# Attention's 32 modulation tiles on VectorE instead of TensorE, values and sums taken out by ScalarE, division by pairs of heads

## The reference, cut to what matters

```python
silu_c, silu_cc = jax.nn.silu(c), jax.nn.silu(c_ctx)
for layer in range(DEPTH):
    mod = jnp.split((silu_c @ w_mod[layer] + b_mod[layer])[:, None, :], 6, axis=-1)
    mod_c = jnp.split((silu_cc @ w_mod[layer] + b_mod[layer])[None, None, :], 6, axis=-1)
    ...
    # attention, 8 heads of 64 values; latents read context and latents, context reads context
    s = jnp.einsum('bhqd,bhkd->bhqk', q, k) * (B_QK ** -0.5)
    p = jax.nn.softmax(s, axis=-1)
    o = jnp.einsum('bhqk,bhkd->bhqd', p, v)
```

## Time and profile before

| | |
|---|---|
| median of 3 runs (lowest to highest) | 5033.49 us (5033.14 to 5033.67) |
| time of the profiled execution | 5033.88 us |
| its span | 5032.0 us |
| TensorE busy over the span | 4360.9 us, 87% |
| VectorE busy over the span | 3626.7 us, 72% |
| ScalarE busy over the span | 1692.8 us, 34% |
| mean granted TensorE clock | 0.902 |
| attention's loop, layer 0 (first maximum of head 0 to the split) | 578.0 to 903.3 us |
| attention's loop, layer 1 | 3364.8 to 3591.2 us |

### The profile page before, as it was taken

How to read it: one execution, slowest core, us unless ns; L and a number is a source line. 1 busy time by engine, 2 the same in 40 slices (tenths; PEclk the granted TensorE clock), 3 DMA queues, 4 the chain that set the end, 5 groups by cost and what they waited for, 6 DMA issues and landing times. The chain is left out here.

```text
span 5032.0 us, 70069 instructions
## 1 busy us (share of the span) xinstructions
PE 4360.9 (87%) x23957; PEld 3683.2 (73%) x23957; DVE 3626.7 (72%) x7107; ACT 1692.8 (34%) x2973; POOL 1018.6 (20%) x1234
## 2 busy tenths in 40 slices
PE   5987699789778999999999969468782799999998
PEld 4877355679767888888888859433461699999998
DVE  1139244379997888898889961734479888989888
ACT  1211432220143333333333332244230344444443
POOL 0000000000394222222222200000000932233232
PEclk9975788887699999999999989569895999999999
DMA  3210011213347888888888831000110499999997
GB/s 121 68 42 1 29 50 55 67 38 102 134 183 269 312 310 322 312 312 310 314 317 312 312 131 55 1 16 1 46 55 17 176 363 363 362 362 363 360 357 288
DMA packets 147967, 957.25 MB, mean 190 GB/s; under 512 B 16945, under 2 KB 17009, under 8 KB 52737
## 3 DMA queue, kind: packets, MB, share of 16 engines
q0 software_dynamic: 82400, 537.66, 28.9%
q1 hardware_dynamic: 65376, 417.36, 22.7%
HBM read 898.30 MB, written 56.62 MB: 190 GB/s over the span
## 5 line engine op out<-in xcount | busy, mean ns | idle before, releaser
L444 PE MATMUL psA<-h_hi,split_hi 128*128 128x512 f32 (+2 forms) x2816 | 996.0, 354 | 109.2 <-DVE h_lo L1623 64.6
L444 PE MATMUL psA<-h_lo,split_hi 128*128 128x512 f32 (+2 forms) x2816 | 988.4, 351 | 0.0
L444 PE MATMUL psA<-h_hi,split_lo 128*128 128x512 f32 (+2 forms) x2816 | 988.1, 351 | 0.0
L1605 DVE TENSOR_TENSOR split_lo<-raw,split_hi 128x1024 fp32r<-128x1024 f32 x596 | 730.9, 1226 | 296.8 <-ACT split_hi L1188 292.4
L1150 POOL DMA_INDIRECT rows<-rows,pick_i x448 | 552.0, 1232 | 1049.4 <-DVE y_tok L2154 966.8
L444 PEld LDWEIGHTS psA<-h_hi,split_hi 128*128 128x128 f32 x2816 | 533.9, 190 | 172.6 <-DVE h_lo L1623 66.2
L1188 ACT ACTIVATE split_hi<-raw 128x1024 fp32r<-128x1024 f32 x596 | 624.8, 1048 | 81.8 <-PE psV L444 74.8
L444 PEld LDWEIGHTS psA<-h_lo,split_hi 128*128 128x128 f32 x2816 | 534.0, 190 | 59.3
L444 PEld LDWEIGHTS psA<-h_hi,split_lo 128*128 128x128 f32 x2816 | 533.1, 189 | 60.4
L2154 DVE SCALAR_TENSOR_TENSOR y_tok<-rows,pick_w,y_tok 128x1024 f32<-128x1024 f32 x444 | 566.8, 1277 | 0.2
L2142 DVE CUSTOM_DVE_ANT_1 rows<-rows,h_tok 128x1024 f32<-128x1024 f32 x448 | 547.6, 1222 | 25.5 <-DMA rows<-rows,pick_i 15.2
(11 more groups left out here) (282 smaller groups left out, 7260.0 us busy)
## 6 DMA issues: line engine op xcount, KB each, us to landing
raw<-expert_pairs SPq DMA_DIRECT2D x256, 1024.0 KB, 7.6
gates<-g_buf SPq DMA_DIRECT2D x26, 2048.0 KB, 6.4
raw<-tiles SPq DMA_DIRECT2D x84, 512.0 KB, 3.6
raw<-mod_tiles SPq DMA_DIRECT2D x80, 512.0 KB, 3.6
g_in<-gates POOLq DMA_DIRECT2D x64, 512.0 KB, 8.5
g_in<-gates POOLq DMA_DIRECT2D x64, 320.0 KB, 5.1
mod_w<-mod_pairs SPq DMA_DIRECT2D x8, 1024.0 KB, 17.9
rows<-rows,pick_i POOLq DMA_INDIRECT x448, 8.4
```

Source lines behind the costliest of these rows:

```text
L444: ins = nc.tensor.matmul(out_, lhsT, rhs, start=start, stop=stop)
L1605: V.tensor_tensor(split_lo[:, n % SPLIT].rearrange("p k n -> p (k n)"), raw[:, n % RAW, :], split_hi[:, n % SPLIT].rearrange("p k n -> p ( ...
```

## The change: where the tiles are multiplied, and who empties the accumulators

- TensorE's four modulation tiles per turn of attention go. VectorE's new `modulate` does a tile with two instructions of 128 partitions by 1024 elements, one for each silu vector: they multiply a weight row per partition with a vector that stands in all partitions, and sum. For that the host lays these 32 tiles out turned, and 128 copies of the two condition vectors (1 MB, `cond_rows`) are loaded by GpSimd's queue behind `w_uq`; ScalarE puts them through Silu once (L1432 of the kernel after), between `k_sq` and `project_q(0)`.
- `take_out(h)` on ScalarE copies sums and values of head h out of PSUM (2 instructions for 512 latents, in layer 0 another 2 for 256 context tokens) and raises `acc_free`. It stands behind the first `exponent` of head h+1.
- `divide(hp)` on VectorE takes the reciprocal of the sums of two heads at once, from SBUF, in all 128 partitions, and multiplies. It stands at the end of the turns h = 2, 4 and 6 and behind the loop.
- `evacuate` is gone in both layers. Between the last `row_max` and `project` there is now one `modulate` in layer 0, and nothing in layer 1.

```diff
@@ -352,7 +355,10 @@
     k_raw = place("k_raw", [P, T], F32, HL + 6144)
     h_rt = place("h_rt", [P, 2, T], F32, HL + 9216)
     b_rt = place("b_rt", [P, 2, T], F32, HL + 9216)
-    sums_inv = place("sums_inv", [P, NLAT], F32, HL + 15360)
+    sums = place("sums", [P, T], F32, HL + 15360)
+    cond_r = place("cond_r", [P, 2, D], F32, SH + 18432)
+    mod_prod = place("mod_prod", [P, D], F32, SH + 18432 + 8192)
+    mod_sum = place("mod_sum", [P, MOD_OWN, 2], F32, SH + 18432 + 12288)
     mix_r = in_r("mix_r", 0, [P, 2, T], F32R)
 
     keysT = in_r("keysT", 67328, [P, WQ_TILES, P])
@@ -739,14 +745,9 @@
                         ins.then_inc(pt_used, 1)
                         seen.n[pt_used] += 1
 
-            mods = [0]
-
-            def modulate(h):
-
-                if l == 0 and h >= 0:
-                    i = mods[0]
-                    mods[0] += 1
-                    mod_tile(psV[:, 1, NCTX + 2 * i:NCTX + 2 * i + 2], (OUT0[l] + MOD_FRONT + i) % RAW)
+            if l == 0:
+                for b in range(RAW):
+                    seen.n[raw_landed[b]] += 16 * MOD_OWN // RAW
 
             pe.wait_ge(psum_V_free, seen.n[psum_V_free] + 4)
             project_q(0)
@@ -768,7 +769,6 @@
                     values(h, s1, n1, 0, (0, 1))
                 if later:
                     project_k(h + 2)
-                modulate(h)
                 if now:
                     turned_scores(h, s1, n1, 2)
...
@@ -776,26 +776,21 @@
                     scores(h + 1, s1, 0)
                 if now and context:
                     turned_scores(h, 0, NCTX, 0)
-                modulate(h)
                 if now:
                     values(h, s1, n1, 1, (0, 1))
                 if after:
                     scores(h + 1, s1, 1)
                 if later:
                     square_sums(h + 2)
-                modulate(h)
                 if after:
                     scores(h + 1, s1, 2)
                     if context:
                         if now:
                             values(h, s1, n1, 2, (0, 1))
                         scores(h + 1, 0, 0)
-                    modulate(h)
                     scores(h + 1, s1, 3)
-                else:
-                    modulate(h)
-                    if context:
-                        values(h, s1, n1, 2, (0, 1))
+                elif context:
+                    values(h, s1, n1, 2, (0, 1))
                 last = (0, NCTX, 0) if context else (s1, n1, 2)
                 if now:
                     values(h, *last, (0,))
@@ -1097,6 +1092,8 @@
             pool.wait_ge(c_done, seen.upto(c_done))
             pool.dma_start(bc[64:96], rope).then_inc(rope_landed, 16)
             pool.dma_start(w_uq[:], bw[l]).then_inc(bw_landed, 16)
+            if l == 0:
+                pool.dma_start(cond_r[:], cond_rows).then_inc(cond_landed, 16)
             pool.wait_ge(mix_ready, seen.upto(mix_ready))
             pool.dma_start(keysT[:], keys[l]).then_inc(keys_landed, 16)
 
@@ -1417,6 +1414,23 @@
                 act.wait_ge(psum_A_free, seen.upto(psum_A_free, 2))
                 act.sem_inc(max_ready, 1)
 
+            def take_out(h):
+
+                r = slice(64 * (h % 2), 64 * (h % 2) + 64)
+                others = slice(64 - 64 * (h % 2), 128 - 64 * (h % 2))
+                if h % 2 == 0 and h:
+                    act.wait_ge(pair_divided, l * BH // 2 + h // 2)
+                act.wait_ge(pt_used, pairs_before + (h + 1) * PT_PAIRS[l] // BH)
+                for b, (s, n, _) in enumerate(own):
+                    A(sums[r, s:s + n], psV[others, b, 0:n], ACT.Copy)
+                    ins = A(mixF[r, 2 + h // 2, s:s + n], psV[r, b, 0:n], ACT.Copy)
+                ins.then_inc(acc_free, 1)
+                act.wait_ge(acc_free, 2 + l * BH + h)
+
+            if l == 0:
+                act.wait_ge(cond_landed, 16)
+                A(cond_r[:], cond_r[:], ACT.Silu).then_inc(cond_rows_ready, 1)
+                act.wait_ge(cond_rows_ready, 1)
             project_q(0)
             project_k(0)
             roots()
@@ -1425,6 +1439,8 @@
                 now, after, later = h >= 0, h + 1 < BH, h + 2 < BH
                 if now:
                     exponent(NLAT)
+                    if h:
+                        take_out(h - 1)
                     exponent(NLAT)
                 if later:
                     project_q(h + 2)
@@ -1437,6 +1453,7 @@
                     roots()
                 if after:
                     max_row(h + 1)
+            take_out(BH - 1)
             act.wait_ge(head_ready, seen.upto(head_ready))
             if l == 0:
                 for b in range(RAW):
@@ -1884,51 +1901,65 @@
                 V.tensor_reduce(dst, src, AX.X, ALU.max, negate=True).then_inc(negmax_ready, 1)
                 dve.wait_ge(negmax_ready, seen.upto(negmax_ready))
 
-            pairs = [0 if l == 0 else PT_PAIRS[0]]
-
-            def evacuate(h):
-
-                r = slice(64 * (h % 2), 64 * (h % 2) + 64)
-                sums = slice(64 - 64 * (h % 2), 128 - 64 * (h % 2))
-                for b, (s, n, _) in enumerate(own):
-                    pairs[0] += (NTT if s else NCTX // P) // 2
-                    dve.wait_ge(pt_used, pairs[0])
-                    V.reciprocal(sums_inv[r, 0:n], psV[sums, b, 0:n]).then_inc(dve_chain, 1)
-                    dve.wait_ge(dve_chain, seen.upto(dve_chain))
-                    ins = V.tensor_tensor(mixF[r, 2 + h // 2, s:s + n], psV[r, b, 0:n], sums_inv[r, 0:n], ALU.mult)
-                    if b == len(own) - 1:
-                        ins.then_inc(acc_free, 1)
-                        dve.wait_ge(acc_free, seen.upto(acc_free))
-                    else:
-                        ins.then_inc(dve_chain, 1)
-                        dve.wait_ge(dve_chain, seen.upto(dve_chain))
-
-            seen.n[acc_free] = 1 + BH * l
+            def divide(hp):
+
+                dve.wait_ge(acc_free, 1 + l * BH + 2 * hp + 2)
+                V.reciprocal(sums[:, t0:T], sums[:, t0:T]).then_inc(dve_chain, 1)
+                dve.wait_ge(dve_chain, seen.upto(dve_chain))
+                o_ = mixF[:, 2 + hp, t0:T]
+                V.tensor_tensor(o_, o_, sums[:, t0:T], ALU.mult).then_inc(pair_divided, 1)
+                dve.wait_ge(pair_divided, seen.upto(pair_divided))
+
+            mods = [0]
+
+            def modulate(h):
+
+                if l or h < 0:
+                    return
+                i = mods[0]
+                mods[0] += 1
+                slot = (OUT0[l] + MOD_FRONT + i) % RAW
+                w = raw[:, slot, :]
+                if i == 0:
+                    dve.wait_ge(cond_rows_ready, 1)
+                dve.wait_ge(raw_landed[slot], seen.upto(raw_landed[slot], 16))
+                V.tensor_tensor_reduce(mod_prod[:], w, cond_r[:, 0], 1.0, 0.0, ALU.mult, ALU.add, mod_sum[:, i, 0:1])
+                V.tensor_tensor_reduce(w, w, cond_r[:, 1], 1.0, 0.0, ALU.mult, ALU.add, mod_sum[:, i, 1:2]).then_inc(mod_passed, 1)
+                dve.wait_ge(mod_passed, MOD_FRONT + i + 1)
+
+            if l == 0:
+                for b in range(RAW):
+
+                    seen.n[raw_landed[b]] += 16 * MOD_FRONT // RAW
             project(0, 0)
             project(0, 1)
             for h in range(-1, BH):
 
                 if h + 1 < BH:
-                    for q in range(3):
-                        row_max(0, q)
+                    row_max(0, 0)
+                    modulate(h)
+                    row_max(0, 1)
+                    modulate(h)
+                    row_max(0, 2)
                     if len(own) > 1:
                         row_max(1, 0)
                     row_max(0, 3)
-                if h >= 0:
-                    evacuate(h)
+                else:
+                    modulate(h)
+                    modulate(h)
+                modulate(h)
                 if h + 2 < BH:
                     project(h + 2, 0)
                     project(h + 2, 1)
+                modulate(h)
+                if h > 0 and h % 2 == 0:
+                    divide(h // 2 - 1)
+            divide(BH // 2 - 1)
             if l == 0:
-                dve.wait_ge(mod_passed, MOD_FRONT + MOD_OWN)
                 n = slice(MOD_FIRST + MOD_FRONT, MOD_FIRST + MOD_FRONT + MOD_OWN)
-                V.tensor_tensor(mod[:, n, :], psV[:, 1, NCTX:NCTX + 2 * MOD_OWN].rearrange("p (n j) -> p n j", j=2),
-                                bm[:, n].unsqueeze(2).broadcast_to([P, MOD_OWN, 2]), ALU.add).then_inc(dve_chain, 1)
+                V.tensor_tensor(mod[:, n, :], mod_sum[:], bm[:, n].unsqueeze(2).broadcast_to([P, MOD_OWN, 2]),
+                                ALU.add).then_inc(dve_chain, 1)
                 dve.wait_ge(dve_chain, seen.upto(dve_chain))
-            if l == 0:
-                for b in range(RAW):
-
-                    seen.n[raw_landed[b]] += 16 * (MOD_FRONT + MOD_OWN) // RAW
 
         def mix_split(l):
             t0 = segs_of(l, False)[-1][0]
     mod_tiles = mods[MOD_FIRST:]
```

(10 more changed lines are left out.)

## The result

| | before | after |
|---|---|---|
| median (lowest to highest), us | 5033.32 (5032.31 to 5033.67), 4 runs | 4966.83 (4962.39 to 4971.94), 4 runs |
| profiled execution, its span, us | 5033.88, 5032.0 | 4962.39, 4960.5 |
| mean granted clock | 0.902 | 0.907 |

The ratio of after to before is 0.9868 [0.9856, 0.9881]: faster by 66.5 us. Forecast were 4925 us and a range of 4910 to 4966; the median lies 41.8 us above the one and 0.8 us above the other's end.

What follows compares the result with a forecast made beforehand. TensorE was taken to set the pace, slowed by modulation tiles, the `q_rot` wait and half clock. Layer 0's -77.9 and layer 1's -31.7 summed to -109.6 us, giving 4925 us, range 4910 to 4966.

Steps and rivals of the forecast that it cites:

- The step that failed: Layer 0's turns: `take_out` frees the accumulators 7.6 us into a turn, TensorE needs them at 8.6, so no wait.
- four ordinary turns, layer 0: Layer 0's turns without a division: 29.4 us each by walking through the products at full clock, against 41.8 before.
- turns h = 3 and 5: Layer 0's turns with `divide` before the first maximum: maximum 2 us late, costing TensorE 0.7; 30.1 us each.
- seventh turn: Layer 0's turn with no head left to project: 25.5 us against 30.9, a gain of 5.4.
- end of the loop: Layer 0, last maximum to split: VectorE sets it with tiles and two divisions, 26.7 us against 28.3, -1.6.
- five turns, layer 1: Layer 1, without `evacuate` ahead of `project`: each costs what h = 0 costs, 23.85 us; 147.9 becomes 119.3, -28.6.
- turn h = 6, layer 1: Layer 1's turn h = 6 loses a 1.78 us wait for `head_ready` and the half clock behind it, -4 us.
- Silu: ScalarE ahead of the first `q_raw`: table load and Silu of the vectors take 3.3 us, less a 1.36 wait, +1.9.
- rival D: Layer 0: VectorE itself sets the pace if its new sums run slowly; at 5 us each 5117 us; chance 0.02.
- B: Both layers: TensorE's clock doesn't come back, the slow share stays; about 4965 us; chance 0.20, half of it included.
- C: Layer 0: VectorE's tiles between maxima, or a `divide`, hold up the scores each turn; 4954 us; chance 0.11.
- E: The change doesn't do what it says, for instance layer 1's wait moves to `take_out`; 2 us per turn, 4947; chance 0.08.

Runs made afterwards that it cites:

- experiment 1: Two buffers for the sums in turn, on the change, so `take_out` waits for the division two pairs back; 4928.1 us, ratio 0.9794 to the kernel before.
- experiment 2: One sums buffer as in the change, but each division one turn earlier, at the end of the odd turns; 4932.34 us, ratio 0.9805 to the kernel before.
- experiment 5: Silu of the vectors moved into ScalarE's first turn, on top of experiment 1; 4926.44 us, ratio 0.9796 to the kernel before.
- experiment 7: On top of experiment 3, all four modulation tiles of a turn in one place behind the square sums; 5018.6 us, ratio 0.9979 to the kernel before.
- experiment 3: Modulation tiles back on TensorE at their four places, all else as in experiment 2; 4987.48 us, ratio 0.9916 to the kernel before.
- experiment 6: On top of experiment 5, tiles spread anew: none behind `project` in h = 2 and 4, two in h = 0, 1, 3, 5; 4924.39 us, ratio 0.9794.

## Why the prediction was wrong

**The step that failed** is the sentence "`acc_free` is raised at 7.6, while TensorE needs it at 8.6 ... no wait". It walks `take_out` by its place in ScalarE's queue and its copies alone. For even heads the diff gives it a wait for `pair_divided`, raised by `divide`, and I had myself put `divide` late, ahead of the first maximum of the turns 3 and 5. Followed through, the walk would have given `take_out(2)` at 2.4 + 6.8 + 2.4 + 6 = 17.6 us behind the last maximum, not at 5.6 (the trace has 17.7). Layer 1's sentence, "`take_out` ends at 6.1 where TensorE needs it at 7.1", fails in the same way. By the walk's own numbers the waits come to some 33 us (an estimate: 11.0 twice, 4 in the last turn, 3.6 twice in layer 1); with the half clock behind them experiment 1 measures 38.7. It removes this wait alone and lands at 4928.1, 3 us from the forecast (5 by its ratio).

Term by term (forecast, measured in the change; us):

| term | forecast | measured | |
|---|---|---|---|
| four ordinary turns, layer 0 | 29.4 each | 29.0 to 29.1 | right |
| turns h = 3 and 5 | 30.1 each | 42.5 (30.25 in 1) | the failed step, +24.8 |
| seventh turn | 25.5 | 25.8 (26.1 in 1) | right |
| end of the loop | 26.7 | 32.4 (26.7 in 1) | the failed step, +5.7 |
| five turns, layer 1 | 119.3 | 128.7 (119.3 in 1) | the failed step, +9.4 |
| turn h = 6, layer 1 | -4 | -3.8 (-2.6 in 1) | near by chance: without the wait it is -2.6 |
| end, layer 1 | +0.9 | +1.2 (+1.5 in 1) | near |
| Silu | +1.9 | about +3.5 | mis-sized: the clock behind it |

**Right besides.** The new sums take 1.22 us, with 0.08 for the read, and the next starts 1.15 later; the reciprocal of 768 elements takes 4.95:

```profile
L1926 DVE CUSTOM_DVE_ANT_0 mod_prod<-raw,cond_r 128x1024 f32<-128x1024 f32 x32 | 39.2, 1225 | 2.0 <-DVE qn L1889 1.1
...
L1907 DVE RECIPROCAL sums<-sums 128x768 f32<-128x768 f32 x4 | 19.8, 4953 | 5.8 <-ACT mixF L1426 5.7
```

So there is nothing for rival D. The waits for maxima that the tiles' removal uncovers, put at 1.0 and 0.7 us, are 0.85 and 0.69 in TensorE's timeline (the first is a maximum of 0.69 us and 0.16 for both hand-overs together, where the walk took 0.15 for each):

```profile
797.35 1.56 PE L450 MATMUL psV<-kn,qn 96*128 96x512 f32 x4 [0.85 <-DVE small L1901]
...
800.03 1.47 PE L450 MATMUL psA<-cst,small 128*1 128x128 f32 x12 [0.69 <-DVE small L1901]
```

The wait for `q_rot` is gone (the longest of its weight loads' waits is 0.5 us). One product of the prediction is off: 41.8 x 0.30 / 2 is 6.3 and not 6.1. The forecast doesn't rest on it, since it took the walk's 29.4 and 30.1 and not the subtraction.

**The rivals.** B is refuted: the clock is 1.00 in every ordinary turn and 0.99 over the loop of experiment 1. What lies below 1.00 in the change's turns stands in the waits for `take_out` and behind them. That B's 4965 lies 2 us from the measured time is chance. C is refuted in the form given (inner tiles hold up no maximum by 2.4 us); a division does make VectorE late in the short seventh turn, as experiment 2 shows. E had the right place (the wait moves to `take_out`, `acc_free` comes too late) with the wrong mechanism: I priced it as 2 us in all turns, since I asked only how long its copies take. It is 10.9 us in two turns, 6.65 in the last and 3.6 in two turns of layer 1, and comes from a wait for another engine. It got 0.08; at its true price of 39 us it would have stood at 4964.

**The mean of the loop hides it.** The clock of 0.96 and VectorE's 157 busy us of 236 look like rival C. Only the turns one by one show four at the forecast and two far off it.

One thing is not settled. Layer 1's experts, whose code no kernel here touches, take a different time in each profiled execution. ScalarE's last `g_buf` row of the groups by line, of the change and of experiment 5 (first and last start):

```profile
L1515 ACT ACTIVATE g_buf<-psA x208: 597/597/600, 1306.2 to 3943.6; 128x512 f32<-128x512 f32 x104
```

```profile
L1516 ACT ACTIVATE g_buf<-psA x208: 597/597/600, 1269.8 to 3899.5; 128x512 f32<-128x512 f32 x104
```

From it to the end of the span are 1016.9 us (4960.5 - 3943.6) in the change and 1028.2 (4927.7 - 3899.5) in experiment 5; before 1022.9, in experiment 1 1022.1. So the profiled execution of experiment 5 reaches both splits 6.1 us before that of experiment 1, and both end at 4927.7. And the change misses its forecast by 43 us in attention (3.2 up to the first maximum, 29.6 in layer 0's loop, 10.1 in layer 1's) and by 2.1 between the two, but by 38.1 at the end, since 6.9 come back behind layer 1's split. These are single profiled executions; what sets the stage's time was not tried.

## What to carry to other kernels

- Where work is moved to another engine and handed over through one buffer, walk both directions: when the consumer may start, and when the producer may write again. The second wait stands on the producer, and what queues behind it there (here an exponent and, through the accumulators, all of TensorE) pays. Where a step is batched by pairs, the buffer must hold two batches, or the batch be consumed before the next begins; 3 KB per partition were worth 39 us.
- Where one piece of work covers a wait, taking either away alone gives little, and both together more than the sum: in layer 0 29.8 and 14.5 us alone, 80.0 together.
- The last turns of a software pipeline have less work. Something that is nearly free in an ordinary turn (a division, 1.1 us) is on the path there (6 us).

## What the runs showed of the hardware that was not expected

- TensorE's clock falls within and behind runs of products with 2 columns, without a gap: 0.50 while the profile shows the engine busy for 2.00 of 2.00 us (experiment 7), 0.92 over a loop with no wait for `q_rot` (experiment 3), 1.00 in the change's ordinary turns, which are without them. It is not the loads (the two windows of experiment 7); what it is about these products no run here shows. "TensorE: Matmul & The Clock Gate" (section "What's actually happening") of the Trainium skill lets the gate follow how busy TensorE has lately been; with busy as the profile counts it, the traces disagree. In experiment 3 the tiles cost 6.8 us of time and 3.0 of clock per turn.
- A wait can cost more than its length: ahead of the loop an idle time of 5.03 in place of 3.13 us left the clock at 0.50 for longer and cost 1.6 us on top of its 1.9.
- The clock doesn't follow a short wait alone: behind the same wait of 1.81 us four products of 128x512 took 1.98 us in experiment 1 and 3.21 in experiment 6.
- A table load's successor starts 1.30 us after it in the new place too (the Silu: 556.06 to 557.36 by the change's timeline of ScalarE), and the instruction ahead of the load ends at 556.04, so the draining that "ScalarE: Activation LUTs" (section "What ACT_TABLE_LOAD costs") adds, about 1.38 us, did not appear here either.
